# An MLP's products back to the model's width as seven block products in place of eight, in three of four quarters

## The reference

```python
def sq_relu_mlp(h, w_up, w_down):
    u = jnp.einsum('btd,df->btf', h, w_up)
    return jnp.einsum('btf,fd->btd', jnp.square(jax.nn.relu(u)), w_down)
...
        m = rms_norm_2(h, norm_mlp[l])
        h = h + jnp.square(jax.nn.relu(m @ w_up[l])) @ w_down[l]
```

## Time and profile before

| | us |
|---|---|
| median of 3 runs | 2275.36 |
| lowest, highest | 2271.13, 2276.34 |
| the profiled execution | 2276.16 |
| its span, first to last instruction | 2274.4 |
| TensorE busy in it | 2174.8 (96%) |
| VectorE, ScalarE, GpSimd busy in it | 1056.4, 766.8, 333.5 |

### The profile page before, as it was taken

One profiled execution on the slowest core, in us unless ns is written; L12 is line 12 of the kernel. 1 busy time (PEld: TensorE's weight loads), 2 busy tenths in 40 slices (PEclk: granted clock), 3 DMA queues, 4 the chain that ended last, 5 costly groups with the idle time before them and its releaser, 6 DMA issues.

```text
span 2274.4 us, 26637 instructions
## 1 busy us (share of the span) xinstructions
PE 2174.8 (96%) x10983; PEld 1721.4 (76%) x10987; DVE 1056.4 (46%) x1590; ACT 766.8 (34%) x1254; POOL 333.5 (15%) x308
## 2 busy tenths in 40 slices
PE   6988888999999999999999999999999999999998
PEld 5765557888888777678888888766778768888887
DVE  3568853433333446754333336355656425333333
ACT  3215453432232334444322323233423314323222
POOL 2210000211010011101110103011145320201000
PEclk9989999999999999999999999999999999999999
DMA  5430001332232221113322233221121213232221
GB/s 140 114 93 20 20 1 56 99 105 93 94 106 97 78 74 56 38 56 102 110 94 93 93 104 108 83 62 46 56 56 56 75 67 110 93 106 96 95 93 74
DMA packets 163507, 182.61 MB, mean 80 GB/s; under 512 B 19702, under 2 KB 123563, under 8 KB 163387
## 3 DMA queue, kind: packets, MB, share of 16 engines
q1 hardware_dynamic: 161066, 174.11, 24.5%
q0 software_dynamic: 2320, 6.80, 1.2%
HBM read 177.75 MB, written 2.17 MB: 79 GB/s over the span
## 4 chain that ended last, share of the span: by engine, by line
PE 86%; DVE 8%; ACT 3%; issue 2%; DMA 1%; SPq 1%; POOL 0%; POOLq 0%; ACTq 0%; DVEq 0%
PE banks L367 70%; PE banks L2519 2%; DVE wl L345 2%; ACT wh L341 2%; PE banks L1272 1%; PE banks L1192 1%; PE banks L1308 1%; PE banks L2638 1%; DVE uTl L537 1%; PE banks L1716 1%; PE banks L1778 1%; PE banks L2209 1%; PE banks L2288 1%; PE banks L1640 1%; PE banks L2259 1%
## 5 line engine op out<-in xcount | busy, mean ns | idle before, releaser
L367 PE MATMUL banks<-uTh,wh 128*128 128x512 f32 (+1 forms) x1408 | 554.2, 394 | 14.1 <-DVE wl L345 4.2
L367 PE MATMUL banks<-uTl,wh 128*128 128x512 f32 (+1 forms) x1408 | 539.0, 383 | 0.0
L367 PE MATMUL banks<-uTh,wl 128*128 128x512 f32 (+1 forms) x1408 | 538.9, 383 | 0.0
L345 DVE TENSOR_TENSOR wl<-stg,wh 128x2048 fp32r<-128x2048 f32 (+1 forms) x154 | 355.4, 2308 | 382.6 <-ACT wh L341 381.9
L367 PE MATMUL banks<-wh,hTr 128*128 128x512 f32 x1696 | 530.5, 391 | 0.3 <-DVE hTr L1838 0.3
L341 ACT ACTIVATE wh<-stg 128x2048 fp32r<-128x2048 f32 (+1 forms) x154 | 293.0, 1903 | 431.6 <-PE banks L367 399.7
L367 PEld LDWEIGHTS banks<-wh,hTr 128*128 128x128 f32 x1696 | 318.9, 188 | 66.7 <-issue 0.7
L367 PE MATMUL banks<-wl,hTr 128*128 128x512 f32 x848 | 330.5, 390 | 0.0
L367 PEld LDWEIGHTS banks<-uTh,wh 128*128 128x128 f32 x1408 | 268.0, 190 | 70.9 <-issue 10.3
L367 PEld LDWEIGHTS banks<-uTh,wl 128*128 128x128 f32 x1408 | 267.2, 190 | 52.5
L367 PEld LDWEIGHTS banks<-uTl,wh 128*128 128x128 f32 x1408 | 268.1, 190 | 50.2 <-issue 2.4
...
## 6 DMA issues: line engine op xcount, KB each, us to landing
stg<-mlp_w_up SPq DMA_DIRECT2D x32, 1024.0 KB, 5.3
stg<-mlp_w_down SPq DMA_DIRECT2D x32, 1024.0 KB, 5.0
stg<-w_in SPq DMA_DIRECT2D x20, 1024.0 KB, 5.2
stg<-w_up SPq DMA_DIRECT2D x16, 1024.0 KB, 5.3
stg<-w_down SPq DMA_DIRECT2D x16, 1024.0 KB, 5.0
...
stg<-even_cmp_w SPq DMA_DIRECT2D x4, 1024.0 KB, 5.5
stg<-odd_w_in SPq DMA_DIRECT2D x4, 1024.0 KB, 5.1
```

The source lines that it names most:

```text
L345: dve.tensor_tensor(lo, stage_of(k), hi.bitcast(F32), ALU.subtract).then_inc(*v_lo.next(k))
L367: t = pe.matmul(outp, x, y, start=(start and k == 0 and m == 0), stop=(stop and k == n - 1 and m == 2))
```

## The change

A quarter's hidden tiles form a matrix of 512 tokens x 1024 columns, and its part of the weights is 1024 x 1024. In quarters 0 to 2 both are cut into 2 x 2 blocks and multiplied with seven block products in place of eight (Strassen's scheme in Winograd's form). The blocks a11 to a22 of the hidden matrix are tokens 0 to 255 or 256 to 511 by even or odd tiles j, so that a pair n of tiles (j = 2g and 2g + 1 of quarter q, n = 4q + g) holds a part of all four. The sums are s1 = a21 + a22, s2 = s1 - a11, s3 = a11 - a21, s4 = a12 - s2 and, of weights, t1 = b12 - b11, t2 = b22 - t1, t3 = b22 - b12, t4 = t2 - b21. Each product is 256 tokens x 512 x 512: 2 token tiles, 4 tiles of the sum and 3 matmuls, 24 in all. The order is that of `SEVEN`: a11 b11, s1 t1, s2 t2, s4 b22, a12 b21, s3 t3, a22 t4. The order of stages becomes up 0, down 0, up 1, down 1 and so on, the fourth quarter's down stage stays as it was, but follows its up stage at once.

GpSimd makes the s of every pair (128 x 256 each) and the four t of every quarter (128 x 2048 each), and adds what has been collected of the products into `h` (12 operations of 128 x 512 a quarter). VectorE now squares, makes a low part of a, b, s1 with s2, and s3 with s4 of each pair, and of seven weight blocks where it had four; it adds products 2, 3 and 5 into two kept sums, and 4 and 6 into `h`, from PSUM. ScalarE makes the high parts that go with them and copies products 0 and 1 out of PSUM. One block, b22, has a staging buffer of its own (`third`), and t1 and t3 share a buffer (`SA`), t2 and t4 another (`SB`).

The diff, cut to its core:

```diff
+        SEVEN = [("a11", (0, 0), 0), ("s1", "t1", 1), ("s2", "t2", 2), ("s4", (1, 1), 3), ("a12", (0, 1), 0), ("s3", "t3", 1),
+                 ("a22", "t4", 2)]
+        BLOCKS = [(0, 0), (1, 1), (1, 0), (0, 1)]
...
+            c = SEVEN[key[4]][1]
+            if c in ("t1", "t2", "t3", "t4"):
+                return (SB if c in ("t2", "t4") else SA), g_sum.at(key[0:3] + (c,))
...
+            v = {"a": RA[n % 2], "b": RB[n % 2], "s12": s12, "s34": s34}[what]
+            c, k = {"a": (3, 2) if last else (0, 1), "b": (1, 2), "s12": (3, 2), "s34": (5, 2)}[what]
...
+        def pe_seven(pe, tag, q):
+            for m, (combo, _, pair) in enumerate(SEVEN):
+                key = (tag, "down", q, "P", m)
+                wh, wl = take(pe, key)
+                c, what = COMBO[combo]
...
+                for ps in ((0, 1, 2), (3,)):
+                    for t in range(2):
+                        s = slice(t * 128, t * 128 + 128)
+                        for p in ps:
+                            pe.wait_ge(*v_up.at((tag, q * 4 + p, what)))
+                            x = products(pe, seven_bank(tag, m, t), [(HC[0][:, p, c, s], HC[1][:, p, c, s], wh[:, p, :], wl[:, p, :])],
+                                         p == 0, p == 3)
...
+            dve.tensor_tensor(r, r, r, ALU.mult).then_inc(*v_up.next((tag, "square", q, j)))
...
+                pool.tensor_tensor(s34[:, 0:o], a[:, 0:o], a[:, o:], ALU.subtract).then_inc(*g_up.next((tag, n, "s3")))
...
+            pool.tensor_tensor(s12[:, 0:o], a[:, o:], b[:, o:], ALU.add).then_inc(*g_up.next((tag, n, "s1")))
+            pool.wait_ge(*g_up.now())
+            pool.tensor_tensor(s12[:, o:], s12[:, 0:o], a[:, 0:o], ALU.subtract).then_inc(*g_up.next((tag, n, "s2")))
+            pool.wait_ge(*g_up.now())
+            pool.tensor_tensor(s34[:, o:], b[:, 0:o], s12[:, o:], ALU.subtract).then_inc(*g_up.next((tag, n, "s4")))
...
+                t = pool.tensor_tensor(SA, block(1, 0), block(0, 0), ALU.subtract)
...
+                t = pool.tensor_tensor(SB, block(1, 1), SA, ALU.subtract)
...
+                pool.wait_ge(*v_lo.at(key + ("P", 1)))
+                pool.wait_ge(*g_sum.at(key + ("t2",)))
+                t = pool.tensor_tensor(SA, block(1, 1), block(1, 0), ALU.subtract)
...
+                pool.wait_ge(*v_lo.at(key + ("P", 2)))
+                t = pool.tensor_tensor(SB, SB, block(0, 1), ALU.subtract)
...
+                if m in (4, 6):
+                    hc = h_part(t if m == 4 else 2 + t, 0)
+                    dve.wait_ge(*g_add.at((tag, q, 0 if m == 4 else 5, t)))
+                    dve.tensor_tensor(hc, hc, b, ALU.add if m == 4 else ALU.subtract).then_inc(*v_add.next((tag, q, m, t)))
+                else:
+                    v = kept_sum(0 if m == 5 else m % 2, t)
+                    dve.wait_ge(*g_add.at((tag, q, {2: 0, 3: 1, 5: 2}[m], t)))
+                    dve.tensor_tensor(v, v, b, ALU.add).then_inc(*v_add.next((tag, q, m, t)))
...
+                for r, c in {0: ((0, 0),), 1: ((1, 1),), 2: ((0, 1),), 3: ((0, 1),), 5: ((1, 1), (1, 0))}[m]:
+                    hc = h_part(2 * r + t, c)
+                    x = pool.tensor_tensor(hc, hc, v, ALU.add)
...
+            for q in range(4):
+                yield from pe_up(pe, tag, src, q)
+                if q < 3:
+                    yield from pe_seven(pe, tag, q)
...
+                act_relu(act, tag, n, 1)
+                for m in range(len(SEVEN) if q < 3 else 0):
+                    split("act", (tag, "down", q, "P", m))
+                    if m == 0:
+                        rest(n)
+                    if m in (1, 2):
+                        act_keep_product(act, tag, q, m - 1)
+                    yield
...
+                dve_square(dve, tag, n, 1)
+                for m in range(len(SEVEN) if q < 3 else 0):
+                    if m > 2:
+                        dve_product(dve, tag, q, m - 1)
+                    split("dve", (tag, "down", q, "P", m))
+                    if m == 0:
+                        rest(n)
+                    yield
...
+                    if g == 3:
+                        pool_t(pool, tag, q, "t1")
+                    pool_s(pool, tag, n, "s3")
+                    if g == 3:
+                        pool_t(pool, tag, q, "t2")
+                    pool_s(pool, tag, n, "rest")
+                    yield
+                pool_product(pool, tag, q, 0)
+                pool_t(pool, tag, q, "t3")
+                pool_product(pool, tag, q, 1)
+                pool_t(pool, tag, q, "t4")
+                for m in (2, 3, 5):
+                    pool_product(pool, tag, q, m)
```

More of the change, by code:

```diff
@@ L274, in build @@
                     for g in range(2):
-                        tm_piece((tag, "down", q, c, g), down, q * 8 + g * 4, c * 512)
+                        rows_q = ins[down][q * 1024:(q + 1) * 1024, c * 512:(c + 1) * 512]
+                        piece((tag, "down", q, c, g), 4, 512, [
+                            (whole, rows_q.rearrange("(k two p) n -> two p k n", two=2, p=128)[g])])
+                if q < 3:
+                    for m in range(len(SEVEN)):
+                        piece((tag, "down", q, "P", m), 4, 512, [])
         for g in range(8):
@@ L298, in build, with is_block, stage_no @@
                 tm_piece(("y", br, g), wname, 0, g * 512, raw=True)
-        ORDER, SPLITS = [], []
+        ORDER, TAKES, SPLITS = [], [], []
+        def is_block(key):
+            return key[1] == "down" and key[2] < 3
+        def stage_no(key):
+            if is_block(key) and key[3:] == (1, 1):
+                return 2
+            return [k for k in ORDER if not (is_block(k) and k[3:] == (1, 1))].index(key) % 2
         def stage_of(key):
             kts, ncols, _, _ = SPEC[key]
-            return STG[ORDER.index(key) % 2][:, 0:kts * ncols]
+            return (STG + [third])[stage_no(key)][:, 0:kts * ncols]
         def halves_of(key):
@@ L314, in take @@
             if Signal.counting:
-                ORDER.append(key)
+                TAKES.append(key)
+                if key[3:4] != ("P",):
+                    ORDER.append(key)
+                elif key[4] == 0:
+                    ORDER.extend(key[0:3] + c for c in BLOCKS)
                 if not raw:
@@ new lines, in act_hi @@
+        def act_hi(act, tag, n, what):
+            if what in ("a", "b"):
+                act.wait_ge(*v_up.at((tag, "square", n // 4, n % 4 * 2 + (what == "b"))))
+            else:
+                act.wait_ge(*g_up.at((tag, n, "s2" if what == "s12" else "s4")))
+            if n >= 4 and n % 4 == 0 and what == "a":
+                act.wait_ge(*p_mm.at((tag, n // 4 - 1, 6, 1)))
+                act.wait_ge(*g_add.at((tag, n // 4 - 1, 5, 1)))
+            v, hi, lo = pair_parts(n, what)
+            act.activation(hi, v, ACT.Copy).then_inc(*a_up.next((tag, n, what)))
@@ new lines, in act_mlp, with rest @@
+        def act_mlp(act, tag, norm):
+            def rest(n):
+                if n >= 0:
+                    for what in ("b",) if n >= 12 else ("s12", "b", "s34"):
+                        act_hi(act, tag, n, what)
+            for q in range(4):
+                for g in range(4):
+                    n = q * 4 + g
+                    if g:
+                        act_relu(act, tag, n - 1, 1)
+                    split("act", (tag, "up", q, g))
+                    if g:
+                        rest(n - 1)
+                    act_relu(act, tag, n, 0)
+                    act_hi(act, tag, n, "a")
+                    yield
+                act_relu(act, tag, n, 1)
[6 more added lines that the diff above has]
+                    yield
+            rest(15)
@@ L3004, in act_program @@
             run(act_squares(act))
[L3005 removed]
+            split("act", TAKES[0], 0)
             run(act_norm(act), act_rope(act, r_index))
```

258 lines of the change are left out of this document (172 added, 86 removed).

## The result

The changed kernel takes 2404.16 us (2397.47 to 2406.16) beside 2275.53 us for the kernel before on the same chip: ratio 1.0564, interval 1.054 to 1.0589. That is 128.6 us slower where 44.6 us slower was forecast; the direction was right, the size was not, and the time lies outside the range of 2278 to 2345.

A forecast was written before the change was run, and what follows sets the result against it. TensorE alone was taken to bound the MLPs; 49.0 us of matmuls removed against stalls of 10.4 us in each of nine quarters (93.6 us) gave +44.6 us on 2276.2, say 2321 us; range 2278 to 2345.

The forecast's parts named there:

- What is removed: Products back: 168 matmuls a quarter in place of 192, 5.44 us in each of nine quarters, 49.0 us gained.
- Sizes of the added operations: On GpSimd: 4.70 us for a block sum t of 2048 elements, 0.69 us for an s of 256.
- First bunch: TensorE's second product waits for the split of t1, behind t2 and the last square: 4.6 us a quarter.
- The clock hides nothing there: Inside the MLPs the granted clock is 1.00; a matmul was costed at 0.2267 us throughout.
- the forecast's second bunch: TensorE's third product waits for t2's split, behind ScalarE's high parts: 1.9 us a quarter.
- the third and fourth: Fifth product waits for its split behind t3, 0.2 us; sixth waits for t3's split behind t4, 3.7 us a quarter.
- Who comes first goes first: VectorE and GpSimd, both reading SBUF, are served in the order they ask; together 79 us in a quarter of 81.6.
- more than forecast: Rival: a split loses its turn to two GpSimd additions as well, +23 us, 2344; chance 0.03.
- The signs that were named: Splits' mean 2.6 to 3 us, TensorE idle about 90 us before products back, squares about 5 us, matmul pace 0.2267 us.
- K: Theory of the experiments, not the prediction: GpSimd keeps the shared port while its next operation is ready, so splits wait.

The follow-up runs named there:

- The version with 11.0 us of gaps and full clock: Changed kernel with all four block sums t moved from GpSimd to VectorE and the squares from VectorE to ScalarE: 2240.17 us, ratio 0.9835.
- the clock held by fillers: Changed kernel with 16 matmuls of no use ahead of each quarter's second product, none at the fourth: 2386.31 us, ratio 1.0497.
- The kernel with the three waits: Changed kernel with GpSimd waiting for its own last operation after t3, between the first product's additions and before t4: 2335.27 us, ratio 1.0251.

## Why the prediction was right and wrong

**What is removed, right.** The version with 11.0 us of gaps and full clock takes 2240.17; less those gaps it is 2229, against 2277.93 - 49.0 = 2228.9 for the removal alone (single executions of either kernel differ by more than these two). The loads, the new buffers and SP's waits cost nothing that shows: no group of products back waits for a transfer.

**Sizes of the added operations, right.** t was put at 4.70 us; t2 to t4 measure 4.48 to 4.86, and t1 5.13. The 4497 ns of the Trainium skill (GPSIMD Engine Reference, 3.1 Elementwise) are near the lower end.

**First bunch, right.** 4.6 us forecast, 4.69 measured, by the operations that were named (t2, the square, the split of t1), and with t2 moved away it falls to 1.8 us.

**The clock, the first step that failed.** "The clock hides nothing there" was true of the kernel before and was carried over to one with gaps of 5 us. The granted clock falls to 0.50 within the first gap, for 6.8 us, and within the second, for 10 to 14 us; in all that is 42.4 us, a term that the sum lacked. It also made the order of the later bunches wrong: the second product at half clock leaves TensorE no reason to wait for the third (the forecast's 1.9 us are absent), and frees its buffer so late that the fourth split asks just after t3 in place of 3.8 us before it. With the clock held by fillers, the forecast's second bunch is there (1.48 us), and in five of nine quarters the third and fourth too. In the run with t2 on VectorE the fourth split came behind t3 in the five quarters with a half-clock stretch ahead of it, and in no other.

**"Who comes first goes first", the second step that failed, and the larger one.** It holds between two single operations, and the Trainium skill (SBUF — State Buffer, Who interferes with whom) says the same in its words on issue order. It did not hold against the run of ready GpSimd operations that begins with t3: the fourth split asked before two additions and t4 started, and went after them. The kernel with the three waits is the one in which the forecast's rule is made true; it takes 2335, 14 us over the forecast. The other 69 of the 83 us that were missed go with this step (12.6 of them as half clock behind the longer gaps). The two steps are not independent: without the half clock ahead of it the fourth split is not passed over, but with the clock held at the first gap alone other splits are, and the time is 2386, 65 us over the forecast. The rival "more than forecast" had the mechanism, a split that loses its turn to two additions, but without t4 behind them, at 2.5 us a quarter and a chance of 0.03; the second gap measured 9.4 to 10.1 us.

**The signs that were named.** Splits with a mean of 2.6 to 3 us and single ones of 3.5 to 6: 2.49 us for those of blocks in `stg`, and nine of 13.0 us each. Squares of about 5 us beside t2: right, 5.15 us in all nine quarters. Idle time of about 90 us in pieces of 4.6, 1.9 and 3.7: 129.4, in pieces of 4.7 and 9.4 to 10.1. TensorE's pace in a product of 0.2267 us: wrong, half of that pace behind each gap.

**Open.** What decides whether VectorE gets in between two ready GpSimd operations is not settled; that the run behind t3 shut it out is shown, why is not (last section).

## What to carry to other kernels

Where VectorE and GpSimd share work on SBUF, adding up both engines' time is not enough: see which VectorE operation TensorE waits for, and do not rely on its getting in between GpSimd operations that are ready one behind the other. Give such sums to the engine on the path (2.3 to 3.4 us each on VectorE, and no split was passed over there) and take load off that engine elsewhere, or break the run with waits on GpSimd's own last operation. And count a new gap of 5 us in TensorE with the slower matmuls that follow it, here a third on top of the idle time.

## What the runs showed of the chip

Counted over the traces of all the kernels above, the one before included: a VectorE operation with both inputs in SBUF asks while a GpSimd operation runs (at least 0.15 us before its end); how often is it let in at that operation's end?

| GpSimd's next operation | VectorE had waited | let in |
|---|---|---|
| starts 0.08 to 0.31 us after that end, behind a wait | 0.16 to 7 us | 509 of 509 |
| ready | under 1.25 us | 356 of 358 |
| ready | 1.25 to 1.6 us | 46 of 64 |
| ready, and the operation that ends is t4 | 3.3 to 4.0 us | 17 of 17 |
| ready, and the operation that ends is t3 | 3.6 to 4.7 us | 0 of 22 |
| ready, and VectorE was already passed over once | 2.5 us and more | 0 of 77 |

So a gap of 0.08 us on GpSimd was enough every time, and who had been passed over once stayed out until there was a gap or the run ended. But that the next operation is ready is not enough to shut VectorE out, as K has it: behind t4, with ready additions next, it always got in. Behind t3 it was let in only where it asked some 1.3 us before t3's end, and there in 12 of 23 cases, at the same lead (1.27 and 1.29 us in the two quarters shown). This may be why that kernel's executions lie 27 us apart; only one of them has a trace. No run here tells what decides it.
